# Forgetting attention: the decay as two rounded rows per head, picked by a K=64 stationary matrix, in place of a table and a matrix of ones

## The reference, cut to what matters

```python
def forgetting_attention(h, w_in, b_f, w_out):        # 16 heads of 64, S = 256
    proj = h @ w_in                                   # q, k, v, and 16 forget columns
    log_f = jax.nn.log_sigmoid(proj[..., 3072:] + b_f)
    c = jnp.cumsum(log_f, axis=1)                     # one row of 256 per head
    s = einsum('bqhd,bkhd->bhqk', q, k) * 64 ** -0.5 + (c[q] - c[k])
    pr = masked_softmax(s, mask)
    return einsum('bhqk,bkhd->bqhd', pr, v).reshape(B, S, D) @ w_out
```

## Time and profile before

| | |
|---|---|
| median of 3 runs | 3348.68 us (3342.57 to 3350.06) |
| the profiled execution | 3349.37 us, span 3347.5 us |
| mean granted TensorE clock | 0.949 |
| TensorE matmul busy | 3158.6 us (94% of the span) |
| VectorE busy | 1943.1 us (58%) |
| ScalarE busy | 1524.9 us (46%) |
| GpSimd busy | 3.1 us |

### The profile page before, as it was taken

One profiled execution on the slowest core, in us unless ns is written; L12 is line 12 of the kernel. 1 busy time (PEld: TensorE's weight loads), 2 busy tenths in 40 slices (PEclk: granted clock), 3 DMA queues, 4 the chain that ended last, 5 costly groups with the idle time before them and its releaser, 6 DMA issues.

```text
span 3347.5 us, 54641 instructions
## 1 busy us (share of the span) xinstructions
PE 3158.6 (94%) x24022; PEld 3036.8 (91%) x24022; DVE 1943.1 (58%) x2298; ACT 1524.9 (46%) x2043; POOL 3.1 (0%) x8
## 2 busy tenths in 40 slices
PE   8899998899999999899999999998999999999899
PEld 8799997899979999799999987988999998898899
DVE  4555556554555555555465677644665568664564
ACT  5543455433444335533443564543434356454433
POOL 0000000000000000000000000000000000000000
PEclk9999888999999989999899999998999999999999
DMA  7245441255424545245355443533555544353453
GB/s 251 101 150 184 137 151 51 91 187 167 135 93 139 188 144 167 86 147 183 114 192 179 151 139 105 158 100 127 195 177 170 185 140 139 112 157 101 135 193 101
DMA packets 388201, 487.36 MB, mean 146 GB/s; under 512 B 33020, under 2 KB 334283, under 8 KB 387708
## 3 DMA queue, kind: packets, MB, share of 16 engines
q1 hardware_dynamic: 386828, 476.50, 43.8%
q0 software_dynamic: 848, 6.32, 0.5%
q10 hardware_dynamic: 288, 1.05, 0.1%
HBM read 480.63 MB, written 3.18 MB: 145 GB/s over the span
## 4 chain that ended last, share of the span: by engine, by line
PE 83%; DVE 10%; ACT 5%; issue 2%; DMA 0%; DVEq 0%; ACTq 0%; SPq 0%
PE ps L387 25%; PE ps L388 24%; PE ps L389 24%; DVE wl L370 3%; PE ps L455 2%; ACT wh L360 2%; DVE ar L2046 1%; DVE ar L966 1%; DVE sm L971 1%; PE ps L1019 1%; PE ps L2195 0%; PE ps L464 0%; PE ps L1018 0%; PE ps L1027 0%; PE ps L2194 0%
## 5 line engine op out<-in xcount | busy, mean ns | idle before, releaser
L370 DVE TENSOR_TENSOR wl<-raw,wh 128x2048 fp32r<-128x2048 f32 x456 | 1036.3, 2277 | 768.3 <-ACT wh L360 768.0
L387 PE MATMUL ps<-ah,wh 128*128 128x256 f32 x4232 | 1225.7, 290 | 30.3 <-DVE al L504 13.7
L388 PE MATMUL ps<-al,wh 128*128 128x256 f32 x4232 | 1217.5, 288 | 0.0
L389 PE MATMUL ps<-ah,wl 128*128 128x256 f32 x4232 | 1216.4, 287 | 0.0
L360 ACT ACTIVATE wh<-raw 128x2048 fp32r<-128x2048 f32 x456 | 863.8, 1900 | 630.1 <-PE ps L389 624.8
L387 PEld LDWEIGHTS ps<-ah,wh 128*128 128x128 f32 x4232 | 834.0, 197 | 35.2 <-issue 28.5
L388 PEld LDWEIGHTS ps<-al,wh 128*128 128x128 f32 x4232 | 834.0, 197 | 0.1
L389 PEld LDWEIGHTS ps<-ah,wl 128*128 128x128 f32 x4232 | 832.9, 197 | 0.0
L387 PE MATMUL ps<-ar_r,wh 128*128 128x256 f32 x2368 | 690.5, 292 | 51.2 <-DVE ar_r L2571 20.7
L388 PE MATMUL ps<-ar_r,wh 128*128 128x256 f32 x2368 | 685.4, 289 | 0.0
L389 PE MATMUL ps<-ar_r,wl 128*128 128x256 f32 x2368 | 685.0, 289 | 0.0
(11 more groups left out here) (363 smaller groups left out, 2651.6 us busy)
## 6 DMA issues: line engine op xcount, KB each, us to landing
raw<-in_ffn_w SPq DMA_DIRECT2D x264, 512.0 KB, 4.3
raw<-in_mlp_w SPq DMA_DIRECT2D x256, 512.0 KB, 4.3
raw<-in_w_in SPq DMA_DIRECT2D x124, 512.0 KB, 4.6
raw<-in_da_w_in SPq DMA_DIRECT2D x48, 512.0 KB, 4.7
raw<-in_ple_gate_w SPq DMA_DIRECT2D x32, 512.0 KB, 4.4
raw<-in_w_ssd_out SPq DMA_DIRECT2D x32, 512.0 KB, 4.7
raw<-in_fox_w_in SPq DMA_DIRECT2D x24, 512.0 KB, 4.7
raw<-in_nsa_w_in SPq DMA_DIRECT2D x20, 512.0 KB, 5.1
```

The costliest lines, as they stand in the source:

```text
L370: nc.vector.tensor_tensor(wl[:, slot, 0:sizes[n]], raw[:, slot, 0:sizes[n]], wh[:, slot, 0:sizes[n]].bitcast(F32), ALU.subtract).then_inc( ...
L387: nc.tensor.matmul(o, wa, xa, start=start, stop=False)
L388: nc.tensor.matmul(o, wa, xb, start=False, stop=False)
L389: return nc.tensor.matmul(o, wb, xa, start=False, stop=stop)
```

## The change

- The stationary matrix of ones goes. In its place `fsel`, one 128x128 matrix for each j, in fp32r: of its 64 rows for head c it picks two. Its rows are built from the identity by three additions (`fpk`, 8 columns) and one copy that spreads each column over 128.
- The table `fcm` of 16 x 256 columns goes. In its place `fcl`, one row of 256 per head, twice: the running sum rounded to fp32r, and 32 partitions further the rest that the rounding left. Both exist for each half of the partitions.
- L1018 becomes a matmul with K=64 (the partitions of head c), in fp32r on both sides. L1019 stays as it is.
- `fcl` no longer lies on `bias`, so the write of `bias`, its read back and the waits for both go; so does the memset of `fc`.
- The construction of `fsel` and the zeros of `fcl` stand at the start of `dve_fox`, ahead of the nine `dve_lo`.

```diff
-        bias_kept = nc.dram_tensor("bias_kept", [P, H64 * S], F32, kind="Internal").ap()
-        fcm = view(ar, 6144, [P, H64, S])
...
                 if fox:
-                    nc.tensor.matmul(o, ones[:, :], fcm[:, 2 * j + c, keys], start=True, stop=False)
+                    nc.tensor.matmul(o, fsel[lo, j, :], fcl[lo, keys], start=True, stop=False)
                 return nc.tensor.matmul(o, qk[lo, j % 8, 0, qs], keys_of(j)[lo, keys], start=not fox, stop=True)
...
-            e.wait_ge(s_mixa, 3)
-            e.dma_start(bias_kept, bias.rearrange("p h k -> p (h k)")).then_inc(s_scr, 16)
-            e.wait_ge(s_scr, 32)
...
+        fsel = view(ar_r, 0, [P, 8, P])
+        fcl = view(ar_r, 1024, [P, S])
+        fpk = view(ar, 11264, [P, 8])
...
+            nc.vector.tensor_tensor(fpk, ident[:, 0:16:2], ident[:, 32:48:2], ALU.add).then_inc(s_d, E.adds(s_d))
+            for at in (65, 97):
+                E.eng.wait_ge(s_d, E.sofar(s_d))
+                nc.vector.tensor_tensor(fpk, fpk, ident[:, at:at + 16:2], ALU.add).then_inc(s_d, E.adds(s_d))
+            nc.vector.tensor_scalar(fcl[:, :], mask[:, :], 0.0, None, ALU.mult)
+            E.eng.wait_ge(s_d, E.sofar(s_d))
+            nc.vector.tensor_copy(fsel[:, :, :], fpk.unsqueeze(2).to_broadcast([P, 8, P])).then_inc(s_d, E.adds(s_d))
             for _ in range(9):
                 dve_lo(E)
...
-            nc.vector.memset(fc[:, :], 0.0).then_inc(s_d, E.adds(s_d))
-            E.eng.wait_ge(E.last, E.sofar(E.last))
             nc.vector.tensor_tensor_scan(fc[h, :], onesw[h, :], fm[h, :], 0.0, ALU.mult, ALU.add).then_inc(s_d, E.adds(s_d))
             E.eng.wait_ge(E.last, E.sofar(E.last))
             nc.vector.tensor_scalar(fc[h, :], fc[h, :], -8.0, None, ALU.mult).then_inc(s_d, E.adds(s_d))
             E.eng.wait_ge(E.last, E.sofar(E.last))
-            E.eng.wait_ge(s_scr, E.next(s_scr, 32))
-            nc.vector.tensor_tensor(fcm[:, :, :], fc[:, :].unsqueeze(1).to_broadcast([P, H64, S]),
-                                           ident[:, 0:H64].unsqueeze(2).to_broadcast([P, H64, S]), ALU.mult).then_inc(s_go, E.adds(s_go))
+            for at in (0, 64):
+                nc.vector.tensor_copy(fcl[at:at + H64, :], fc[h, :]).then_inc(s_d, E.adds(s_d))
+            E.eng.wait_ge(E.last, E.sofar(E.last))
+            for at in (32, 96):
+                last = nc.vector.tensor_tensor(fcl[at:at + H64, :], fc[h, :], fcl[h, :].bitcast(F32), ALU.subtract)
+            last.then_inc(s_go, E.adds(s_go))
...
-        def pool_bias_again(E):
-            E.eng.wait_ge(s_x, 24 * 2 + 8)
-            E.eng.dma_start(bias.rearrange("p h k -> p (h k)"), bias_kept).then_inc(s_rows, 16)
...
-                    else:
-                        E.eng.wait_ge(s_rows, E.next(s_rows, 16))
```

More of the change, by code:

```diff
@@ L2666, in _ @@
             pool_start(E)
-            pool_bias_again(E)
         @block.tensor
```

## The result

| | before | after |
|---|---|---|
| median, this comparison (4 and 4 runs) | 3348.93 us (3342.57 to 3350.06) | 3325.70 us (3325.17 to 3326.26) |
| ratio | | 0.9935, 95% interval 0.9917 to 0.9952 |
| again on another chip (22 and 8 runs) | 3350.28 us | 3325.45 us, ratio 0.9943, 0.9922 to 0.9963 |
| the profiled execution | 3349.37 us | 3326.26 us, span 3324.5 |

The kernel became 23.2 us faster where 17.4 were forecast. The two intervals allow 16 to 28 and 12 to 26 us. In the two traces the block of the forgetting layer gave 16.7 us of it, so the forecast is to be tested against the trace rather than the total.

The account below looks back on a forecast made before the run. TensorE was taken to bound the forgetting attention; steps of 3.2 us in place of 6.12 would bring its last transposes from 997.08 to 979.64, gain 17.4, so 3348.68 - 17.4 = 3331.3 us, range 3326 to 3339.5.

Parts of the forecast that it names:

- What bounds the stage: Forgetting attention: TensorE stays the bound by some 0.3 us per step; the VectorE and ScalarE loop needs 2.9.
- The two costs of K=128: Scores: alternating K=128 and K=64 costs a fixed 0.20 us per matmul and loses the overlap of the two heads.
- Change of type: Rival in the scores: switching fp32r and f32 drains TensorE as the K change did; step 5.3, time 3339.2, chance 0.10.
- Transposes, values, entry: Part of each attention step outside the scores, including entry into them: 2.07 us, taken from NSA.
- The scores: Per attention step: 0.92 us for both heads side by side with the change back to K=128, plus 0.23 for new matmuls.
- together 0.23: New decay matmuls per step, two per head, heads side by side: 0.11 us for 128 columns and 0.12 for 256.
- no overlap of heads: Rival in the scores: the heads go one after the other; step 4.1, gain 13.8 us, time 3334.9, chance 0.15.
- The start: First three transposes of the attention, copied from layer 3: 957.56, 960.63 and 964.25, with 0.23 charged for the new matmuls.
- The end: Attention: three steps of 3.2 bring the sixth transposes to 973.85; 5.79 us more bring the last to 979.64.
- VectorE's new work, the earlier decay: Before the scores: 2.0 to 2.5 us of new VectorE work and decay ready 2.5 to 3 us earlier count zero.
- Given back later: Rival after the attention: a stage waiting for transfers or clock phases returns the gain; time 3342 to 3349, chance 0.04.
- The clock: Attention start: a half-clock stretch near 957 to 963, its cost copied from layer 3; 2 us allowed each way.

Follow-up runs that it names:

- e3: The kernel after without the decay matmul, so the decay is left out of the scores; 3327.43 us, ratio 0.9924 to the kernel before.
- e1: The kernel after with the decay matmul reading f32 instead of fp32r, K=64 kept; 3339.88 us, ratio 0.9978 to the kernel before.
- e2: The kernel after with the decay matmul on all 128 partitions (K=128, fp32r), which changes the computation; 3361.88 us, ratio 1.0027 to the kernel before.
- e6: The kernel after with one decay matmul of 384 columns per head in place of two (128 and 256); 3332.83 us, ratio 0.9955.
- e7: The kernel after with one 384-column decay matmul per head, plus 12 and 6 unread matmuls in the idle start; 3329.03 us, ratio 0.9938.
- e8: The kernel after with an f32, K=64 decay matmul, plus 6 and 4 unread matmuls in the idle start; 3341.46 us, ratio 0.9972.
- e9: The kernel after plus 12 and 6 unread fp32r matmuls of 512 columns in the idle start; 3324.22 us, ratio 0.9923.
- e10: Second run of the kernel after with one 384-column decay matmul per head and the idle start filled; 3323.01 us, ratio 0.9925.
- e12: Second run of the kernel before without the bias write, read back and their waits, matmul unchanged; 3349.48 us, ratio 1.0006.
- e4: The kernel before with its decay table moved off bias, without the write, read back and waits; 3347.29 us, ratio 0.9994.

## Why the prediction was right, and where its sizes were off

The forecast was 3331.3 us by a shorter attention stage; 3325.7 was measured, 0.3 us below the range's end at 3326. The mechanism was right in its main steps: TensorE stays the bound, the extra cost of each change between K=128 and K=64 is gone from the scores, and the heads overlap. One sign that it named did not come: the heads' matmuls do not start within a few hundredths of a us of each other. And that the block's 16.7 us lie so near the forecast 17.4 is in part luck: 2.35 us too little was charged and 1.64 us came back elsewhere, as the points below show; the remaining 6.4 us of the measured gain were in no term of the forecast.

- *What bounds the stage.* TensorE before, TensorE after, with some reserve: the loop through VectorE and ScalarE was put at 5.79 us for two steps. In e3 it did not bind at a step of 2.95, and the last two steps, which do wait for ScalarE, took 977.71 - 971.92 = 5.79.
- *The two costs of K=128.* The fixed part and the serial heads. e1 removes K=128 alone and takes 2.06 us off the scores; e2 keeps it and keeps both costs. Rule and rows agree here: the Trainium skill, "TensorEngine Tiling (Array Packing)", section Key Properties, says that a change of the tiling mode drains TensorE. The trace agrees, by e2's 0.42 and 0.62 us per product of q and k, 1.04 for one head, against 0.87 for both heads in e3.
- *Change of type.* It does not drain as the change of K did: with that rival the step would be 5.3 and e1 would beat the kernel after. It is 3.50 against 4.15 in e1.
- *Transposes, values, entry.* 2.08 measured, 2.07 forecast.
- *The scores: the term that was mis-sized.* 0.92 + 0.23 = 1.15 was forecast, 1.41 measured. The q and k part costs 0.87 (e3), so the new matmuls cost 0.54, not 0.23. The step in which it failed is "together 0.23": it charged one head's columns and took the heads as exactly side by side. The 0.11 per matmul was a guess between two bounds, with no row for 128 columns in fp32r, and its reason names a load of 128x128, where the trace has 64x128. In the trace head 1 starts 0.34 behind head 0; without the decay (e3) the heads' single records start 0.01 apart. 0.54 - 0.34 = 0.20 is then near the 0.23. e6, with half as many decay matmuls, has a lag of 0.29 and costs 1.31 - 0.87 = 0.44. The fp32r type is not the reason for the lag: in e1 the columns of one head need 2 x 0.65 = 1.30 us, and the two heads took 2.06; the second starts 0.55 late there (976.92 against 976.37). In both traces its first matmul starts together with the decay matmul of head 0's second half (968.51 and 968.53 after, 976.92 for both in e1); why it does was not tried. So "no overlap of heads" was partly true: 3.50 lies a third of the way from 3.2 to 4.1.
- *The start.* First transposes at 957.85 for 957.56. The stage began 0.38 later in this execution, so this is exact to 0.1 us. The second and third came 4.07 and 8.24 behind the first, where 3.07 and 6.69 were forecast: without the decay matmul they come at 3.06 and 6.46 (e3, transposes at 956.61, 959.67 and 963.07), as in layer 3. So this too is the new matmul. It stands in two sets of scores between these rows, and I had charged it once, at 0.23. The first set runs at clock 0.50 and takes 961.92 - 959.33 = 2.59 us where e3's takes 959.67 - 958.08 = 1.59, so 1.00 more; the second runs at full clock and costs its 0.54; and the second transposes and the values behind them run longer at the half clock, which is worth the last 0.23. That is the 8.24 - 6.46 = 1.78 us, 1.5 more than charged.
- *The end.* From the sixth to the last transposes 5.79 us, as forecast. The last ones came at 982.37; less the 0.38 by which the stage began later, that is 2.35 later than 979.64: 1.46 from the start and 0.89 from the three steps (3 x 0.30).
- *The clock at the end.* Before, the last transposes were slow and the output projection began at 1004.50, 7.42 behind them; after, it began at 988.15, 5.78 behind them. This gives 1.64 back, inside the 2 us allowed. 17.4 - 2.35 + 1.64 = 16.7, the 16.74 of the stretch table.
- *VectorE's new work, the earlier decay.* Nothing, as forecast. VectorE's timeline of the kernel after shows that it still waits for ScalarE behind the new work and at the end:

```profile
891.70 4.58 DVE L368 TENSOR_TENSOR wl<-raw,wh 128x2048 fp32r<-128x2048 f32 x2 [6.26 <-ACT wh L358]
...
951.63 2.29 DVE L368 TENSOR_TENSOR wl<-raw,wh 128x2048 fp32r<-128x2048 f32 x1 [3.63 <-ACT wh L358]
953.84 1.01 DVE L964 SCALAR_TENSOR_TENSOR ar<-ps,mask 128x256 f32<-128x256 f32 x2
```

- *Given back later.* No. Of the eleven other stretches into which I cut the two traces none is longer than before by more than 0.8 us.

**The rest, 23.1 - 16.7 = 6.4 us in the profiled executions.** 4.60 us lie in the one later stage shown above. In the traces of the kernels here this stage takes one of two times, whatever the kernel: 452.7 to 452.9 in before, e1, e7, e8 and e9, and 447.1 to 448.2 in after, e2 to e6, and e10 to e12. e9 differs from after by filler alone and has the long one; e2, with the longest attention, has the short one. So this part of the measured gain is where TensorE's slow stretches happened to fall. Stretches ahead of the change, the same work in every kernel, differ in the same way: the one from 193.2 to 378.0 us takes 184.8 us in before and after, 180.7 in e3 and 189.1 in e8. Runs of one kernel scatter by some 20 us, likely for the same reason. Whether that scatter explains all of the surplus stays open. Over the thirteen comparisons the time moved on average 3.5 us (standard error 1.0) more to the fast side than the attention did. They share five sets of runs of the kernel before, so they are not independent and that error is too small. The surplus goes from -2.5 (e8) to +9.0 (e9), it is near zero in the two kernels that leave the attention alone (e4 2.0, e12 -2.0), and no trace shows a place for it.

**The clock.** The slow stretch after was forecast near 957 to 963 and came at 956.5 to 963.4. That the fall goes with the idle time at the stage's start is shown by e1 against e8, e6 against e7 and e10, and the kernel after against e9: filled, it is gone each time. How long it then lasts is not a matter of that idle time alone: 6.8 us in the kernel after, 20.5 in e6, 23.9 in e1, although TensorE was busy for 19.94 of the 20.50 and 23.38 of the 23.90 us. And e2 fell at 956.7, with work without gaps from 953.54 on and a gap of only 0.69 us ahead of that, and stayed for 64.9 us; the kernel before, with the same alternation of K but f32, ran its steps at 1.00. The Trainium skill, "TensorE: Matmul & The Clock Gate", section "HAM oscillation — how this bites in real kernels", gives the rule that TensorE should have no idle gaps beyond a certain length; e8, e7 and e10 agree in direction, e2 does not: there the clock was held down with no gap at all. What holds it was not found.

## What to carry to other kernels

When small-K matmuls stand between full-K ones, look for the start-to-start time that the columns don't explain and for a second head that waits; giving the odd one out the same K pays for both, here 2.1 of 2.7 us per step, and a cheaper type pays far less alone. Price an added matmul at each clock that the stretch really has, count every place where it stands, and charge the lag of the second head as well as the columns. And test such a forecast on the stage in the trace: with runs that scatter by 20 us from where slow clock stretches fall, a total that is a few us better than the stage has not shown a second mechanism.

## What was not expected of the hardware

- The clock stayed at 1.2 GHz for 64.9 us with TensorE busy for all of them (e2), and for 20.5 and 23.9 us with it busy for 97 and 98% of them (e6, e1).
- 18 matmuls that nobody reads, 4.7 us of TensorE time in the idle start, went with a clock of 1.00 for the whole attention in e7 and e10, which is 8.2 us shorter than e6's (35.6 against 43.8); in e9 and e8 the clock fell later instead, at 979.5 and 989.0.
- One more matmul ahead of the product of q and k, in the same 64 rows and into the same place, delays the other head by 0.29 to 0.34 us (e6, after), and by 0.55 in f32 (e1); without it the two heads' records start 0.01 us apart (e3).
